# Token features read ready-turned from the host, and per-group norms whose shift runs on ScalarE

## What is computed

```python
def rmsnorm(x, g):
    y = x32 * lax.rsqrt(jnp.mean(x32 * x32, axis=-1, keepdims=True) + EPS)
    return (y * g.astype(F32)).astype(x.dtype)

def modulate(xn, shift, scale):
    return xn * (1 + scale) + shift
...
for l in range(DEPTH):
    h = modulate(rmsnorm(x, norm_mix_g[l]), sh1, sc1)
    hc = modulate(rmsnorm(xc, norm_mix_g[l]), csh1, csc1)
    mix, mix_c = token_mixers(h, hc, w_in[l], ...)
    x = x + g1 * (mix @ w_out[l])
    ...
    h = modulate(rmsnorm(x, norm_ffn_g[l]), sh2, sc2)
    # layer 0: dense SwiGLU, layer 1: top-2-of-8 experts
```

## Time and profile before

| | us |
|---|---|
| median of 3 runs | 6993.63 (6993.28 to 6995.26) |
| span of the profiled execution | 6989.3 |
| PE busy | 5804.7 (83%) |
| DVE busy | 2834.6 (41%) |
| ACT busy | 1943.7 (28%) |
| POOL busy | 262.9 (4%) |
| turning stage x0 | 41.27 |
| nm0 / nm1 / nf1, first load issue to the next phase's | 65.76 / 66.10 / 57.98 |
| nf0, same | 61.14 |

### The profile page before, as it was taken

The page is one execution under the profiler, slowest core; times in us unless marked ns, Lnnn a source line. Parts: engine busy times, 40 slices in busy tenths (PEclk is TensorE's granted clock), DMA queues, the critical chain, the costliest instruction groups (busy, mean ns, idle before and its releaser), DMA issues. The chain is left out here.

```text
span 6989.3 us, 78523 instructions
## 1 busy us (share of the span) xinstructions
PE 5804.7 (83%) x32272; PEld 4844.7 (69%) x32273; DVE 2834.6 (41%) x2895; ACT 1943.7 (28%) x1888; POOL 262.9 (4%) x304
## 2 busy tenths in 40 slices
PE   8959937569997969946666999989988999989884
PEld 8934415458887745414456899988977999979874
DVE  0020047431112330037526544456476444465575
ACT  0000011121112220011104433345365333354452
POOL 0020001000000020002010000000000000000000
PEclk9979968789999989967778999999999999999997
DMA  6230110321113331010238655567488555576685
GB/s 202 99 114 26 41 32 1 115 77 59 62 59 125 137 136 34 29 40 1 97 139 304 215 179 183 188 205 255 157 293 293 182 176 187 183 253 210 207 288 190
DMA packets 717348, 1008.52 MB, mean 144 GB/s; under 512 B 58801, under 2 KB 571377, under 8 KB 714353
## 3 DMA queue, kind: packets, MB, share of 16 engines
q1 hardware_dynamic: 687184, 927.48, 39.5%
q0 software_dynamic: 13040, 49.29, 1.9%
q10 hardware_dynamic: 16688, 24.91, 1.0%
HBM read 912.73 MB, written 88.87 MB: 143 GB/s over the span
## 5 line engine op out<-in xcount | busy, mean ns | idle before, releaser
L1805 DVE TENSOR_TENSOR moe_wl<-moe_wst,moe_wh 128x2048 fp32r<-128x2048 f32 x630 | 1420.4, 2287 | 691.2 <-ACT moe_wh L1763 689.0
L1691 PE MATMUL ps<-moe_wh,moe_xh 128*128 128x256 f32 x5152 | 1492.0, 290 | 101.4 <-DVE moe_wl L1805 95.6
L1763 ACT CAST moe_wh<-moe_wst 128x2048 fp32r<-128x2048 f32 x630 | 1175.9, 1903 | 1277.4 <-PE ps L1712 1215.7
L1691 PE MATMUL ps<-moe_wl,moe_xh 128*128 128x256 f32 x5152 | 1472.7, 286 | 0.0
L1691 PE MATMUL ps<-moe_wh,moe_xl 128*128 128x256 f32 x5152 | 1472.0, 286 | 0.0
L1691 PEld LDWEIGHTS ps<-moe_wh,moe_xh 128*128 128x128 f32 x5152 | 1004.1, 195 | 113.7 <-DVE moe_wl L1805 99.5
L1691 PEld LDWEIGHTS ps<-moe_wl,moe_xh 128*128 128x128 f32 x5152 | 1004.8, 195 | 7.1
L1691 PEld LDWEIGHTS ps<-moe_wh,moe_xl 128*128 128x128 f32 x5152 | 1003.2, 195 | 0.0
L1712 PE MATMUL ps<-moe_wh,moe_ah 128*128 128x512 f32 x1288 | 416.1, 405 | 162.4 <-DVE moe_al L1810 162.4
L1299 PE MATMUL ps<-hh,up_wh 128*128 128x512 f32 (+1 forms) x1056 | 376.5, 357 | 51.9 <-DVE up_wl L1343 40.0
L1712 PE MATMUL ps<-moe_wl,moe_ah 128*128 128x512 f32 x1288 | 403.3, 394 | 0.0
(11 more groups left out here) (311 smaller groups left out, 6411.7 us busy)
## 6 DMA issues: line engine op xcount, KB each, us to landing
moe_wst<-in_moe_w_gate SPq DMA_DIRECT2D x210, 1024.0 KB, 7.5
moe_wst<-in_moe_w_up SPq DMA_DIRECT2D x210, 1024.0 KB, 10.0
moe_wst<-in_moe_w_down SPq DMA_DIRECT2D x210, 1024.0 KB, 5.0
ada_w<-in_w_ada SPq DMA_DIRECT2D x24, 2048.0 KB, 8.3
down_wst<-in_ffn_w_down SPq DMA_DIRECT2D x66, 512.0 KB, 3.4
proj_w<-in_w_in SPq DMA_DIRECT2D x8, 2048.0 KB, 7.8
four_dft<-in_dft_seq SPq DMA_DIRECT2D x16, 1024.0 KB, 4.5
xs_d<-route_zero SPq DMA_DIRECT2D x1, 16384.0 KB, 53.4
```

The source lines that it names most:

```text
L1691: x = nc.tensor.matmul(ps[:, 2 * kind + p % 2, i * W:(i + 1) * W], xx[:, k, t], w[:, k, :], start=(k == 0 and j == 0), stop=(k == KD - 1 a ...
L1763: nc.scalar.copy(weights(wh, kind, p), weights(wst, kind, p)).then_inc(hi[kind], 1)
L1805: nc.vector.tensor_tensor(weights(wlo, kind, p), weights(wst, kind, p), weights(wh, kind, p).bitcast(F32), ALU.subtract).then_inc(split[ki ...
```

## The change

Four things, of which the first three are in `phase_norm`, which nm0, nm1 and nf1 run:

- one semaphore per group for the loads, so that group 0 can start when it has landed;
- ACT squares group g+1 before it takes the root of group g;
- the shift moves from POOL (in place in `hT`) to ACT (product in, `hT` out), and DVE writes the product in place into `xT`;
- `phase_to_features` is gone. The host hands over the tokens as `xT`, already laid out as [128, 8, 1280]; nm0 and the output projection of layer 0 read it from that input. `x` and `ctx` are inputs no longer.

```diff
-def phase_to_features(nc, io, S):
...
-def phase_norm(nc, S, name, xT, hT, l, which, groups):
+def phase_norm(nc, S, name, src, xT, hT, l, which, groups):
...
+        xl = [ph.sem(f"x_loaded{g}") for g in range(len(groups))]
...
-                for t0, n in groups:
-                    sp.dma_start(xT[:, :, t0:t0 + n], S["xT_d"][:, :, t0:t0 + n]).then_inc(xl, 16)
+                for g, (t0, n) in enumerate(groups):
+                    sp.dma_start(xT[:, :, t0:t0 + n], src[:, :, t0:t0 + n]).then_inc(xl[g], 16)
...
-                act.wait_ge(xl, 16 * len(groups))
 
                 def squares(g, t0, n):
+                    act.wait_ge(xl[g], 16)
                     for k in range(KD):
                         q = g * KD + k
                         if q >= 4:
                             act.wait_ge(sq_used, q - 3)
                         nc.scalar.activation(sq[:, q % 4, :n], xT[:, k, t0:t0 + n], ACT.Square).then_inc(sq_ready, 1)
 
-                def root(g, t0, n):
+                squares(0, *groups[0])
+                for g, (t0, n) in enumerate(groups):
+                    if g + 1 < len(groups):
+                        squares(g + 1, *groups[g + 1])
                     act.wait_ge(var_ready, g + 1)
                     nc.scalar.activation(rstd[:, g % 2, :n], rstd[:, g % 2, :n], ACT.Sqrt).then_inc(sd_ready, 1)
-
-                for g, (t0, n) in enumerate(groups):
-                    squares(g, t0, n)
-                    root(g, t0, n)
+                    j = 1 if t0 < CTX else 0
+                    for k in range(KD):
+                        act.wait_ge(scaled, g * KD + k + 1)
+                        nc.scalar.activation(hT[:, k, t0:t0 + n], xT[:, k, t0:t0 + n], ACT.Identity,
+                                             bias=mod[:, l, 24 * which + k, j:j + 1]).then_inc(shifted, 1)
+                act.wait_ge(shifted, KD * len(groups))
...
-                            out=hT[:, k, t0:t0 + n], in0=xT[:, k, t0:t0 + n], scalar=gmod[:, l, which, j, k:k + 1],
+                            out=xT[:, k, t0:t0 + n], in0=xT[:, k, t0:t0 + n], scalar=gmod[:, l, which, j, k:k + 1],
...
-            @block.gpsimd
-            def _(pool):
-                for g, (t0, n) in enumerate(groups):
-                    j = 1 if t0 < CTX else 0
-                    for k in range(KD):
-                        pool.wait_ge(scaled, g * KD + k + 1)
-                        nc.gpsimd.tensor_scalar(hT[:, k, t0:t0 + n], hT[:, k, t0:t0 + n],
-                                                mod[:, l, 24 * which + k, j:j + 1], None, ALU.add).then_inc(shifted, 1)
-                pool.wait_ge(shifted, KD * len(groups))
...
-                sp.dma_start(xT[:, :, a:], S["xT_d"][:, :, a:]).then_inc(x_ld, 16)
+                sp.dma_start(xT[:, :, a:], (io["xT"] if l == 0 else S["xT_d"])[:, :, a:]).then_inc(x_ld, 16)
...
-        phase_to_features(nc, io, S)
...
-                    phase_norm(nc, S, f"nm{l}", xT, hT, l, 0, GROUPS)
+                    phase_norm(nc, S, f"nm{l}", io["xT"] if l == 0 else S["xT_d"], xT, hT, l, 0, GROUPS)
...
-                        phase_norm(nc, S, "nf1", xT, hT, l, 1, groups)
+                        phase_norm(nc, S, "nf1", S["xT_d"], xT, hT, l, 1, groups)
...
+def features(ctx, x):
+
+    rows = np.concatenate([np.asarray(ctx)[0], np.asarray(x)[0]], 0)
+    return np.ascontiguousarray(rows.reshape(T, KD, P).transpose(2, 1, 0))
```

More of the change, by code:

```diff
@@ L236, in _ @@
                 dve.wait_ge(mod_done, 1)
-def phase_to_features(nc, io, S):
-    with Phase(nc, "x0") as ph:
-        rows = ph.sb("rows", [P, 2, D])
-        turned = ph.sb("turned", [P, 2, KD, P])
-        loaded = [ph.sem(f"loaded{s}") for s in range(2)]
-        stored = [ph.sem(f"stored{s}") for s in range(2)]
-        tr, ev = ph.sem("transposed"), ph.sem("evacuated")
-        ps, ident = S["ps"], S["c"]("ident")
+def phase_norm(nc, S, name, src, xT, hT, l, which, groups):
+    with Phase(nc, name) as ph:
+        sq = ph.sb("sq", [P, 4, 512])
+        rstd = ph.sb("rstd", [P, 2, 512])
+        xl = [ph.sem(f"x_loaded{g}") for g in range(len(groups))]
+        sq_ready, sq_used, var_ready, sd_ready, scaled, shifted, rst = (
+            ph.sem(n) for n in ("sq_ready", "sq_used", "var_ready", "sd_ready", "scaled", "shifted", "rstd_ready"))
+        ps, ones = S["ps"], S["c"]("ones")
+        gmod, mod = S["gmod"], S["mod"]
         with nc.Block() as block:
@@ L251, in _ @@
             def _(sp):
-                for n in range(NT):
-                    src = io["ctx"][0, n * P:(n + 1) * P, :] if n < NCT else io["x"][0, (n - NCT) * P:(n - NCT + 1) * P, :]
-                    if n >= 2:
-                        sp.wait_ge(tr, n - 1)
-                    sp.dma_start(rows[:, n % 2, :], src).then_inc(loaded[n % 2], 16)
-            @block.tensor
-            def _(pe):
-                for n in range(NT):
-                    pe.wait_ge(loaded[n % 2], 16 * (n // 2 + 1))
-                    if n >= 2:
-                        pe.wait_ge(ev, n - 1)
-                    for k in range(KD):
-                        b = 2 * (n % 2) + k // 4
-                        t = nc.tensor.transpose(ps[:, b, (k % 4) * P:(k % 4 + 1) * P], rows[:, n % 2, k * P:(k + 1) * P], ident)
-                    t.then_inc(tr, 1)
@@ L278, in _ @@
             @block.scalar
             def _(act):
-                for n in range(NT):
-                    act.wait_ge(ev, n + 1)
-                    act.dma_start(S["xT_d"][:, :, n * P:(n + 1) * P], turned[:, n % 2, :, :]).then_inc(stored[n % 2], 16)
-                for s in range(2):
-                    act.wait_ge(stored[s], 16 * (NT // 2))
-def phase_norm(nc, S, name, xT, hT, l, which, groups):
-    with Phase(nc, name) as ph:
-        sq = ph.sb("sq", [P, 4, 512])
-        rstd = ph.sb("rstd", [P, 2, 512])
-        xl, sq_ready, sq_used, ss_ready, var_ready, sd_ready, scaled, shifted, rst = (
-            ph.sem(n) for n in ("x_loaded", "sq_ready", "sq_used", "ss_ready", "var_ready", "sd_ready", "scaled", "shifted", "rstd_ready"))
-        ps, ones = S["ps"], S["c"]("ones")
-        gmod, mod = S["gmod"], S["mod"]
-        first = groups[0][0]
-        with nc.Block() as block:
-            @block.sync
-            def _(sp):
-                for t0, n in groups:
-                    sp.dma_start(xT[:, :, t0:t0 + n], S["xT_d"][:, :, t0:t0 + n]).then_inc(xl, 16)
-            @block.scalar
-            def _(act):
-                act.wait_ge(xl, 16 * len(groups))
@@ L328, in _ @@
                         pe.wait_ge(sq_ready, q + 1)
-                        mm = nc.tensor.matmul(ps[:, g, :n], ones, sq[:, q % 4, :n], start=(k == 0), stop=(k == KD - 1))
-                        mm.then_inc(sq_used, 1)
+                        nc.tensor.matmul(ps[:, g, :n], ones, sq[:, q % 4, :n], start=(k == 0), stop=(k == KD - 1)).then_inc(sq_used, 1)
             @block.vector
@@ L1991 @@
     nc = bacc.Bacc("TRN2", target_bir_lowering=False, num_devices=1)
-    shapes = {"cst": constants(), "dft_seq": dft(SEQ), "dft_ctx": dft(CTX)}
+    shapes = {"xT": features(inputs["ctx"], inputs["x"]), "cst": constants(), "dft_seq": dft(SEQ), "dft_ctx": dft(CTX)}
     arrays, io = {}, {}
```

12 lines of the change are left out of this document (1 added, 11 removed).

## The result

The changed kernel is slower, where the prediction said faster: 7093.55 us (7092.27 to 7096.8, 4 runs) against 6994.44 us for the kernel before (6993.28 to 6996.05, 4 runs), a ratio of 1.0142 (95% interval 1.0127 to 1.0156), 99 us more. Forecast were 6911 us.

What follows compares the result with a forecast made beforehand. Taken as bound by chains of waits in x0 and the norms, not by a full engine; 41.3 + 13.5 + 14.5 + 13.6 - 0.6 = 82.3 us less, 6993.6 - 82.3 = 6911 us, range 6903 to 6921 us.

Steps and rivals of the forecast that it cites:

- the only slower one: Rival in the projections: PE's clock stays at the lower level once x0's PE work goes, 7011 us; chance 0.01.
- Part 1: Turning stage x0: its whole window goes, 41.3 us gained, with nm0's first load 1.55 us after the modulation.
- Part 2: Norms nm0 and nm1, groups of 256, 512, 512: new chain built from nf0's rows, gaining 13.5 and 14.5 us.
- the rival of the doubled switch: ACT's table switch in nm0 and nm1 costs 2 x 1.3 = 2.6 us, total 6914 us; chance 0.06.
- the Trainium skill's drain of about 1380 ns: Rule weighed for ACT's table switch: 2.66 us each, nm0 and nm1 losing a further 1.38 us each, 6914 us.
- nm1 and nf1: Last shifts of these norms 50.2 and 43.1 us after the first load issue, gaining 14.5 and 13.6 us.
- (a): Unknown in the norms: time of ACT's shift with f32 output, 0 to +3 us in all, taken as 0.
- (b): Unknown in the norms: ACT's squares at PE's pace under its lower clock, -1.7 to +1.7 us per norm; nf0's taken.
- (c): Unknown at the norms' ends: ACT finishes last instead of POOL; +0.2 us taken for each of three, up to +1.2.
- (d): Unknown in the norms: POOL and DVE no longer run together; held to be in nf0's rows already.
- The new source: Rival: nm0's three loads from the new source take twice as long, 9 us lost, 6920 us; chance 0.05.
- ScalarE's order: Rival: the norms, bound by something else in nf0, gain only 3.8, 4.8 and 8.1 us, 6936 us; chance 0.06.

Runs made afterwards that it cites:

- best: The changed kernel with the first instruction of PE's experts loop at slot 0 of a 256-instruction block, timed in four runs: 6911.65 us, ratio 0.9878 to the kernel before.
- slot0: The changed kernel with the first instruction of PE's experts loop put at slot 0 of a 256-instruction block, single run: 6906.78 us.
- after_inc174: The changed kernel with 174 semaphore increments, for which nobody waits, on PE at the end of nm0: 6913.18 us.

## Why the prediction was wrong, point by point

**The step that failed** stands in its first paragraph: "nothing else in the program changes, so nothing else can pay much". The sum went only over the stages whose lines change. PE's instructions of x0 were priced by their time (18.52 us of PE, inside a window of 41.27) and not as a piece of PE's instruction stream. Taking out 174 of them moved all later code of PE, and some 3200 us later the experts' loop lay badly against the blocks in which instructions arrive: 184.1 us in place of 0. No rival covered this: the only slower one was about PE's clock in the projections and stood at 0.01, so the case fell in the 0.02 for what wasn't thought of. The sign hung on that one term.

What could have been seen in the profile of before: one branch of 2.19 to 4.27 us in each one-tile unit, where the usual one takes 0.34, in a hardware loop whose body is longer than a block; and a change that takes instructions from the same engine ahead of it. From these rows the term can be estimated: a unit has 15 steps, so if every second branch were as slow as the slowest, 7 stalls of 3.9 us (4.27 less 0.34) in each of seven units, 191 us to lose, and next to nothing to gain, as most branches were quick. That this lies so near the 184 is luck: the slow branches turned out to be six a unit, not seven, and 6 to 7 us long, in part behind matmuls that still ran, and a third of the loss came through the clock. It would have been a rival on the slower side with a real chance.

**Part 1, x0: right.** The modulation's last DVE row is at 367.47 for 0.71 us, nm0's first load at 369.74, 1.56 us later (forecast 1.55). x0 is gone with its 41.3 us.

**Part 2, the chain of nm0: right to 0.2 us.** ScalarE's rows of nm0 in the changed kernel, and SP's first load of the projection:

```profile
375.55 1.33 ACT L265 ACTIVATE nm_sq<-TM 128x256 f32<-128x256 f32 x4 [354.43 <-DMA TM<-in_xT]
...
380.97 2.82 ACT L265 ACTIVATE nm_sq<-TM 128x512 f32<-128x512 f32 x5 [0.72 <-DMA TM<-in_xT]
...
386.38 1.28 ACT L272 ACT_TABLE_LOAD   x1
...
387.68 0.42 ACT L272 ACTIVATE nm_rstd<-nm_rstd 128x256 f32<-128x256 f32 x1
...
390.44 3.30 ACT L276 ACTIVATE hT<-TM,mod 128x256 f32<-128x256 f32 x8 [2.34 <-DVE TM L300]
...
393.64 2.17 ACT L265 ACTIVATE nm_sq<-TM 128x512 f32<-128x512 f32 x4
...
400.52 0.61 ACT L272 ACTIVATE nm_rstd<-nm_rstd 128x512 f32<-128x512 f32 x1
...
405.34 5.36 ACT L276 ACTIVATE hT<-TM,mod 128x512 f32<-128x512 f32 x8 [4.21 <-DVE TM L300]
...
410.60 0.61 ACT L272 ACTIVATE nm_rstd<-nm_rstd 128x512 f32<-128x512 f32 x1
...
415.42 5.36 ACT L276 ACTIVATE hT<-TM,mod 128x512 f32<-128x512 f32 x8 [4.21 <-DVE TM L300]
422.56 1.01 SPq L357 DMA_DIRECT2D proj_w<-in_w_in  x2
```

Counted from the issue at 369.74: first square 5.8 us (forecast 5.6, or 6.3 for the later landings), group 1's squares 11.2 (11.0), root of group 0 at 17.9 (17.35), its shifts end at 24.0 (23.4), root of group 1 at 30.8 (29.9), its shifts end at 41.0 (40.1), root of group 2 at 40.9, the last shift ends at 51.0 (50.2 + 0.7 = 50.9). The figures from group 0's root on are those of the sum without the 0.7 us of nm0's later landings, which closes most of the gap to the measured ones. The third root starts as the shifts of group 1 end and doesn't wait for DVE, as forecast. The table load stands exposed, with no gap: 386.38 + 1.28 = 387.66, and the root starts at 387.68. So neither the rival of the doubled switch nor the Trainium skill's drain of about 1380 ns (ScalarE: Activation LUTs, "What ACT_TABLE_LOAD costs") shows here, with ACT's last square only just done ahead of the load.

**nm1 and nf1: right to 1.1 us, with opposite signs.** Their last shifts in the changed kernel:

```profile
2538.42 5.36 ACT L276 ACTIVATE hT<-TM,mod 128x512 f32<-128x512 f32 x8 [4.21 <-DVE TM L300]
```

```profile
3521.67 5.36 ACT L276 ACTIVATE hF<-xF,mod 128x512 f32<-128x512 f32 x8 [4.21 <-DVE xF L300]
```

nm1 ends 2543.78 - 2492.53 = 51.3 us after its issue (forecast 50.2), nf1 3527.03 - 3484.93 = 42.1 (43.1).

**The unknowns.** (a) The shift with an f32 output takes 5.36 us for eight, as nf0's did with the other type: 0, as taken. (b) The leg of group 2, from the end of group 0's shifts to the next root, took 6.8 us where 6.54 were taken. (c) The end of nm0 took 422.56 - 420.78 = 1.78 us, 0.4 more than behind POOL, where +0.2 was taken. (d) Nothing.

**The rivals.** None of the four happened. The new source is as quick as the old one (nm0's and nm1's windows differ by 0.2 us), ScalarE's order gives nothing back, and the projections are no longer: between nm0 and the routing all stages but nm1 and nf1 together moved by some 0.5 us net.

That best lies within 1 us of the forecast of 6911 is partly luck: it ran on a chip on which the kernel before took 6997.71 us, and its loop stands at another place than that kernel's. Against the kernel before on their own chips, best gains 86.1 us, slot0 82.6 and after_inc174, which puts the old place back, 76.2, where 82.3 were forecast. So the sum was right to some 6 us for the program it had in mind, in which the loop keeps its good place, and the 82.67 us gained up to the routing say it more closely. It doesn't make the prediction right: in the kernel as changed, the place is part of the change.
